# A two-layer decoder trunk: all four tiles of x transposed as loaded, two tiles loaded ahead of the weights, and zero matmuls in PE's waits

## The reference

```python
def rms_norm(x, g):
    y = x * lax.rsqrt(jnp.mean(x * x, axis=-1, keepdims=True) + 1e-6)
    return y * g

for i in range(2):
    hdn = rms_norm(x, norm_g[i])
    q, k, v, z = jnp.split(hdn @ w_in[i], 4, axis=-1)      # (1024, 4096)
    if i == 0:    # block-sparse attention with rotary; q and k normalised per head
        q = apply_rope(rms_norm(split_heads(q), a_q_norm), cos, sin)
        k = apply_rope(rms_norm(split_heads(k), a_k_norm), cos, sin)
        y = moba_attention(q, k, split_heads(v))
    else:         # attention with a forget-gate bias, no rotary
        y = forgetting_attention(q, k, v, log_sigmoid(f_logit))
    x = x + (merge_heads(y) * silu(z)) @ w_out[i]
```

## Time and profile before

| | before |
|---|---|
| median of 3 runs | 550.47 us (550.08 to 550.68) |
| the profiled execution | 551.01 us |
| its span, first to last instruction | 548.9 us |
| PE busy | 539.3 us, 98% of the span |
| DVE, ACT, POOL busy | 406.1, 291.2, 300.2 us |
| chain of waits that ended last | PE 93% of it |
| DMA | 50.09 MB, mean 91 GB/s |

### The profile page before, as it was taken

The page is one execution under the profiler, slowest core; times in us unless marked ns, Lnnn a source line. Parts: engine busy times, 40 slices in busy tenths (PEclk is TensorE's granted clock), DMA queues, the critical chain, the costliest instruction groups (busy, mean ns, idle before and its releaser), DMA issues.

```text
span 548.9 us, 9783 instructions
## 1 busy us (share of the span) xinstructions
PE 539.3 (98%) x2963; PEld 498.1 (91%) x2963; DVE 406.1 (74%) x1049; ACT 291.2 (53%) x863; POOL 300.2 (55%) x352
## 2 busy tenths in 40 slices
PE   5999999999999999999999999999999999999998
PEld 4989999999999999888888999999999999998887
DVE  2886999999999999964563778778787878788331
ACT  5846473737383828272454473838373737474400
POOL 4674555555555555452735486757574747476300
PEclk9999999999999999999999999999999999999999
DMA  8914314141313131324413335425141534232121
GB/s 252 256 14 116 116 39 116 38 116 38 115 38 115 43 110 57 96 80 122 114 40 79 96 97 78 113 61 130 46 131 44 121 57 122 72 102 80 36 96 59
DMA packets 78540, 50.09 MB, mean 91 GB/s; under 512 B 4256, under 2 KB 71720, under 8 KB 78512
## 3 DMA queue, kind: packets, MB, share of 16 engines
q1 hardware_dynamic: 78496, 49.74, 33.6%
q10 hardware_dynamic: 16, 0.00, 0.0%
HBM read 47.62 MB, written 2.11 MB: 91 GB/s over the span
## 4 chain that ended last, share of the span: by engine, by line
PE 93%; POOL 2%; ACT 1%; DMA 1%; DVE 1%; SPq 1%; issue 0%; POOLq 0%
PE banks L380 26%; PE banks L382 26%; PE banks L381 26%; PE banks L510 6%; PE banks L496 3%; PE banks L485 2%; PE banks L484 2%; PE banks L483 2%; DMA first_raw<-in_a_w_in_dram 1%; ACT hT_hi L677 1%; POOL w_lo L1180 1%; PE banks L417 1%; POOL rstd L1207 0%; DVE hT_lo L880 0%; PE banks L537 0%
## 5 line engine op out<-in xcount | busy, mean ns | idle before, releaser
L1180 POOL TENSOR_TENSOR w_lo<-w_raw,w_hi 128x512 fp32r<-128x512 f32 x147 | 189.6, 1303 | 82.7 <-ACT w_hi L645 82.7
L380 PE MATMUL banks<-w_hi,hT_hi 128*128 128x384 f32 x512 | 173.9, 340 | 1.2 <-DVE hT_lo L880 0.6
L381 PE MATMUL banks<-w_lo,hT_hi 128*128 128x384 f32 x512 | 171.8, 336 | 0.0
L382 PE MATMUL banks<-w_hi,hT_lo 128*128 128x384 f32 x512 | 171.8, 336 | 0.0
L966 DVE STREAM_TRANSPOSE banks<-qkn 32x256 f32<-32x256 f32 x240 | 109.4, 456 | 3.6
L380 PEld LDWEIGHTS banks<-w_hi,hT_hi 128*128 128x128 f32 x512 | 96.6, 189 | 3.8 <-POOL w_lo L1180 1.7
L381 PEld LDWEIGHTS banks<-w_lo,hT_hi 128*128 128x128 f32 x512 | 96.6, 189 | 0.6
L382 PEld LDWEIGHTS banks<-w_hi,hT_lo 128*128 128x128 f32 x512 | 96.5, 189 | 0.0
L691 ACT ACTIVATE junk<-banks 128x128 bf16<-128x128 f32 x128 | 34.1, 273 | 117.4 <-PE banks L382 117.4
L645 ACT ACTIVATE w_hi<-w_raw 128x512 fp32r<-128x512 f32 x148 | 89.1, 638 | 9.4 <-PE banks L382 5.4
L1032 DVE RECIPROCAL gz<-gz 128x128 f32<-128x128 f32 x64 | 54.4, 910 | 0.7 <-ACT gz L743 0.7
(11 more groups left out here) (120 smaller groups left out, 906.5 us busy)
## 6 DMA issues: line engine op xcount, KB each, us to landing
w_raw<-in_b_w_in_dram SPq DMA_DIRECT2D x64, 256.0 KB, 3.6
w_raw<-in_a_w_in_dram SPq DMA_DIRECT2D x52, 256.0 KB, 2.9
w_raw<-in_w_out_dram SPq DMA_DIRECT2D x32, 256.0 KB, 2.7
first_raw<-in_a_w_in_dram SPq DMA_DIRECT2D x12, 256.0 KB, 5.4
cos_t<-c_rows SPq DMA_DIRECT2D x8, 256.0 KB, 3.7
out_dram<-xs SPq DMA_DIRECT2D x7, 256.0 KB, 2.0
xs<-in_x_dram SPq DMA_DIRECT2D x3, 512.0 KB, 6.8
xs<-in_x_dram SPq DMA_DIRECT2D x2, 256.0 KB, 3.3
```

Of the source, the lines that this page charges most:

```text
L380: pe.matmul(dst, ah, bh, start=first and m == 0, stop=False)
L381: pe.matmul(dst, ah, bl, start=False, stop=False)
L382: mm = pe.matmul(dst, al, bh, start=False, stop=last and m == n - 1)
L1180: pool.tensor_tensor(w_lo[:, slot, k, :], raw, f32(w_hi[:, slot, k, :]), ALU.subtract).then_inc(wlo_set, by)
```

## The change

UNSCALED goes from 2 to 4: no tile of x is multiplied by r before its transposes, norm_x is gone from layer 0, r_rows has four columns, and scale_z covers 512 columns instead of 256. SP issues both halves of tile 0 and then tile 1 ahead of the first weights. PE transposes tiles 0 and 1 one after the other, with four and then five matmuls on the zeros of wf behind them (keep_busy, into PSUM bank 0, which the first real matmul overwrites), and then takes each chunk for both tiles. ACT turns to tile 0 before chunk 0. DVE takes w_lo of chunks 0, 3 and 5 instead of 3, 5 and 7, POOL 1, 2, 4, 6 and 7 instead of 0, 1, 2, 4 and 6. The folding of the sine tables moves wholly to POOL.

```diff
-UNSCALED = 2
+UNSCALED = 4
+ZEROS = KC * (LO_ROW + 8)
-POOL_FIRST = {0: 1, 1: 1, 2: 2, 4: 2, 6: 2}
-DVE_FIRST = (3, 5, 7)
+POOL_FIRST = {1: 2, 2: 1, 4: 2, 6: 2, 7: 1}
+DVE_FIRST = (0, 3, 5)
@@ SP
                 sp.dma_start(xs[:, 0, cols], x[0, 0:P, cols]).then_inc(x_half[half], 16)
-                load_first((half,))
             load_x(1)
-            load_first(range(2, 6))
+            load_first(range(6))
@@ PE
+            def keep_busy(count):
+                zeros = wf[:, :, :].rearrange("p k n -> p (k n)")
+                for _ in range(count):
+                    pe.matmul(banks[:, 0, 0:ZEROS], zeros[:, 0:P], zeros[:, 0:ZEROS], start=True, stop=True)
...
                     turn_hidden(layer, 0)
-                    first_w(0, 0)
-                    qkv_part(layer, 0, 0, 0, (0,))
+                    keep_busy(4)
                     turn_hidden(layer, 1)
-                    for k in (1, 2):
-                        first_w(0, k)
-                        qkv_part(layer, 0, 0, 0, (k,))
-                    qkv_part(layer, 0, 0, 1, range(3))
-                    for k in range(3, KC):
+                    keep_busy(5)
+                    for k in range(KC):
                         if k == KC - 1:
                             turn_hidden(layer, 2)
                         first_w(0, k)
@@ DVE
-                    norm_x(layer, 2)
-                    split_first_w(0, (7,))
                     split_hidden(layer, 2)
-                    norm_x(layer, 3)
-                    fold_tables()
+                    split_hidden(layer, 3)
+                    dve.wait_ge(tables_set, 1)
+                    fold_cosines()
                     split_v(layer, 0, 0, 0)
                     split_v(layer, 0, 0, 1)
-                    split_hidden(layer, 3)
```

More of the change, by code:

```diff
@@ L310, in load_second @@
                     load_chunk(w_raw[:, k, :], head_src(0, 1)(k), raw_in[k])
-                sp.wait_ge(wlo_set, 4)
-                sp.wait_ge(wlo_odd, 1)
+                sp.wait_ge(wlo_set, 3)
+                sp.wait_ge(wlo_odd, 2)
                 for k in range(RAW, KC):
@@ L747, in first @@
                     act.dma_start(gz[0:KC, 0, 0:P], norm_g[0].rearrange("(k n) -> k n", k=KC)).then_inc(gain_in[0], 16)
+                    act.wait_ge(gain_set, 1)
+                    split_hidden(layer, 0)
                     split_w(layer, 0, 0, (0,))
-                    act.wait_ge(gain_set, 1)
-                    split_half(layer, 0, 0)
+                    split_half(layer, 1, 0)
                     split_w(layer, 0, 0, (1,))
[L752 to L757, removed]
+                    split_half(layer, 1, 1)
+                    split_w(layer, 0, 0, range(2, KC))
+                    split_hidden(layer, 2)
                     square_x(layer, 0)
-                    square_x(layer, 3)
-                    split_hidden(layer, 2)
                     square_x(layer, 1)
+                    split_hidden(layer, 3)
                     read_qkv(layer, 0, 0, 0)
                     read_qkv(layer, 0, 0, 1)
-                    split_w(layer, 1, 1, (0, 1))
-                    split_hidden(layer, 3)
-                    split_w(layer, 1, 1, (2, 3, 4))
+                    for t in (2, 3):
+                        square_x(layer, t)
                     read_qkv(layer, 0, 0, 2)
+                    split_w(layer, 1, 1, range(5))
                     split_w(layer, 1, 1, (5,))
@@ L896, in split_first_w, with fold_cosines @@
                                       ALU.subtract).then_inc(wlo_odd, 1)
[L898 to L908, removed]
+            def fold_cosines():
                 for m in range(2):
@@ L1071, in first @@
                     split_hidden(layer, 0)
+                    split_first_w(0, (0,))
                     split_hidden(layer, 1)
                     split_first_w(0, (3, 5))
-                    norm_x(layer, 2)
-                    split_first_w(0, (7,))
                     split_hidden(layer, 2)
-                    norm_x(layer, 3)
-                    fold_tables()
+                    split_hidden(layer, 3)
+                    dve.wait_ge(tables_set, 1)
+                    fold_cosines()
                     split_v(layer, 0, 0, 0)
                     split_v(layer, 0, 0, 1)
-                    split_hidden(layer, 3)
-                    dve.wait_ge(tables_set, 3)
+                    dve.wait_ge(tables_set, 2)
                     dve.wait_ge(cos_set, 1)
@@ L1087, in first @@
                     norm_qk(layer, 0, 2)
-                    split_first_w(1, (3,))
+                    split_first_w(1, (0,))
                     split_v(layer, 0, 0, 3)
                     norm_qk(layer, 0, 3)
-                    split_first_w(1, (5, 7))
+                    split_first_w(1, (3, 5))
                     dve.wait_ge(wf_split, 1)
@@ L1097, in first @@
                     dve.tensor_scalar(cos_t[:, 0, 0, :], cos_t[:, 0, 0, :], SCALE, None, ALU.mult).then_inc(tables_set, 1)
-                    dve.wait_ge(tables_set, 4)
+                    dve.wait_ge(tables_set, 3)
                     split_v(layer, 0, 0, 0)
@@ L1224, in first @@
                     for k, by in POOL_FIRST.items():
-                        if k == 6:
-                            rstd_x(layer, 2)
                         split_w(layer, 0, 0, (k,), by=by)
-                    for t in (0, 3, 1):
+                    pool.wait_ge(tables_in, 64)
+                    pool.tensor_scalar(gains[:, 0, :], gains[:, 0, :], SCALE, None, ALU.mult).then_inc(tables_set, 1)
+                    for t in range(2):
                         rstd_x(layer, t)
+                    pool.wait_ge(tables_set, 1)
+                    half = P // 2
+                    for m in range(2):
+                        for a in range(2):
+                            folded = pool.tensor_tensor(sin_t[:, :, m, a * half:(a + 1) * half],
+                                                        sin_t[:, :, 1, a * half:(a + 1) * half],
+                                                        bcast(gains[:, m, (1 - a) * half:(2 - a) * half], TILES), ALU.mult)
+                    folded.then_inc(tables_set, 1)
                     rstd_qk(layer, 0, 0)
                     rstd_qk(layer, 0, 1)
[L1233 to L1239, removed]
+                    for t in (2, 3):
+                        rstd_x(layer, t)
                     rstd_qk(layer, 0, 2)
-                    for k, by in tuple(POOL_FIRST.items())[1:]:
+                    for k, by in POOL_FIRST.items():
                         if k == 4:
```

## The result

Over 20 runs the kernel after took 551.99 us in the median (550.25 to 552.76), the kernel before 550.58 us on the same chip: a ratio of 1.002, with a 95% interval of 1.0014 to 1.0026. The predicted 552.0 us was met, but not for the reason given. In 14 of the 20 runs the mean granted clock of TensorE was 0.997, and they took 551.76 to 552.76 us; in the other six it was 1.0, and they took 550.25 to 550.95 us, no more than before. The profiled execution (552.51 us, span 550.4, clock 0.997) is one of the 14, and it shows what lowers the mean: one stretch of 3.4 us at half clock near 40 us (half of 3.4 is 0.3% of the span). Of the runs without a profile only the mean clock is known, and I take 0.997 there for the same event.

The account below looks back on a forecast made before the run. A fixed PE block begins at T, set by POOL and DVE: 19.2 + 4.9 + 12.5 + 1.9 = 38.5, plus 1.6 of collisions, 40.1 against 38.62, so 1.5 us later: median 552.0 us, range 549.8 to 553.8.

Parts of the forecast that it names:

- T2 = 19.2 us (Part 1): Loads and zeros: PE turns to tile 2 of x at 19.2 us, against 20.20 before.
- The zeros at 0 to 0.5 us: Nine zero matmuls during PE's early waits cost nothing; lifting the clock gains 0 to 0.5 us, taken as 0.
- T: Start of the transposes of q and k of head 0, opening the fixed block; predicted 40.1 us against 38.62.
- ACT's row of T2 + 4.9: ACT's hT_hi of tile 2 and squares of tiles 0 and 1 end 4.9 us after PE turns to tile 2.
- POOL's row of 12.5 us and collisions of 1.6 us (Part 2): POOL's factors, sine pieces and low parts before T take 12.5 us; meetings with DVE add 1.6 us.
- the two cancel: Rival: only PE's lead or collision-free POOL and DVE holds, or half of each; T 37.5 to 39.7, 550.9 us, chance 0.30.
- Scale_z and r_row at 0 (Part 3): In the periods, scale_z over 512 columns, at most 0.86 us, is covered by slack; later r_rows cost nothing.
- The clock falls in PE's new pause: Rival: PE idles some 4 us from 35.8, returns at the lower clock, loses 1.9 us; 553.9 us, chance 0.08.

Follow-up runs that it names:

- experiment 2: The kernel after without the nine zero matmuls (keep_busy(4) and keep_busy(5)): 552.31 us, ratio 1.0032.
- experiment 1: The kernel after with 14 unread products of 384 columns filling PE's pause before the transposes of q and k: 550.74 us, ratio 1.0.
- experiment 3: The kernel after with the gains and q's half of the sine table made on DVE, POOL keeping k's half: 549.44 us, ratio 0.9978.
- experiment 8: The kernel of experiment 3 with one reciprocal of 176 columns on DVE ahead of norm_qk(3), lengthening PE's pause: 551.45 us.
- experiment 5: Experiment 3 with ACT reading the last tile's sums earlier, POOL's factor at once, DVE making three low parts of head 1: 549.02 us, ratio 0.9972.
- experiment 9: The kernel after with six unread products of 384 columns in the last part of PE's pause: 550.62 us.
- experiment 6: The kernel after with four unread products of 384 columns at the start of PE's pause: 552.01 us.
- held-up kernel before: The kernel before with 3.5 unread reciprocals on DVE ahead of its normalising of tile 3, giving PE a pause; run twice: 553.02 and 553.09 us.

## Why the prediction was right in its number and wrong in its reason

- **T2 = 19.2 us (Part 1): roughly right.** Measured 18.68. ACT's first high part, so chunk 0, starts at 8.20, not at 8.8, within the bounds given; the first products run at the upper level (0.33 us at 9.87) and wait for POOL's low parts, 0.79 us at 11.89. PE's lead over before is 1.5 us there, and z ends 2.4 us earlier than before (38.58 less the 2.68 of pause is 35.90; 38.62 less 0.28 is 38.34), as predicted, but in part by luck: PE needs 17.2 us from T2 to the end of z, not 16.6, which makes up for a T2 that came 0.5 us early. The working also names 20 products there; the trace has 18, and it is 18 that give its 16.6.
- **The zeros at 0 to 0.5 us: right, taken as 0.** Without them T2 and T are 0.01 and 0.02 us later (experiment 2). They do raise the clock before the first product, and those products wait for low parts all the same, as the prediction had it.
- **ACT's row of T2 + 4.9: right.** ACT's last sum of tile 1 ends at 23.56, T2 + 4.88.
- **POOL's row of 12.5 us and collisions of 1.6 us (Part 2): the step that failed.** Its rows:

```profile
23.64 0.19 POOL L1179 TENSOR_TENSOR msx<-ssx,eps 128x1 f32<-128x1 f32 x1
...
24.59 2.83 POOL L1223 TENSOR_TENSOR sin_t<-sin_t,gains 128x256 f32<-128x256 f32 x4
27.37 0.65 POOL L1194 TENSOR_TENSOR msq<-ssq,eps_raw 128x2 f32<-128x2 f32 x1
28.09 1.03 POOL L1196 TENSOR_TENSOR rstd<-msq,power 128x2 f32<-128x2 f32 x1
...
32.84 2.55 POOL L1169 TENSOR_TENSOR w_lo<-w_raw,w_hi 128x512 fp32r<-128x512 f32 x2
35.35 0.64 POOL L1194 TENSOR_TENSOR msq<-ssq,eps_raw 128x2 f32<-128x2 f32 x1
36.08 0.69 POOL L1196 TENSOR_TENSOR rstd<-msq,power 128x2 f32<-128x2 f32 x1
```

  From 23.64 to 36.77 it is 13.1 us, where 14.1 was predicted. And on DVE, what it met:

```profile
27.01 1.56 DVE L900 TENSOR_TENSOR cos_t<-cos_t,gains 128x512 f32<-128x512 f32 x2
...
34.56 1.39 DVE L894 TENSOR_TENSOR w_lo<-w_raw,w_hi 128x512 fp32r<-128x512 f32 x1
```

  The collisions are there and where they were put, but I priced each as a whole DVE instruction in POOL's way. The sine pieces were over 0.4 us after the first cosine piece began and took 2.83 for four; the small operations behind them lost 0.46 (0.65 for 0.19) and 0.33 (1.03 for 0.70), and the one beside DVE's low part 0.45: 1.2 us, not 1.6. The three factors of x behind it took 0.95 us each (23.64 to 24.59 the first), not 1.13, which is the other 0.6. With T2 0.5 us earlier, T came out at 38.58 and not at 40.1. This is the rival "the two cancel", with its price of 550.9 us; the six runs without the fall (median 550.5) are it. The rule of the Trainium skill ("SBUF — State Buffer", Who interferes with whom) on mutual exclusion agrees with these rows, if read as waiting out what is left of the other's instruction: 0.33 to 0.46 us here. That `norm_qk` disturbs POOL no row shows.
- **Scale_z and r_row at 0 (Part 3): right in effect.** In the first period scale_z takes 1.09 us, above the bound of 0.86 that I gave; the block from T on is as long as before wherever the clock holds (510.3 in experiment 1, 510.4 in experiment 3), so it is hidden.
- **"The clock falls in PE's new pause": weighed at 0.08 and true in 14 of 20 runs.** Its mechanism is the result; its price, 1.9 us, was near the 1.6 measured, and its base, T at 40.1, was the forecast's error. I took the case to need a pause of some 4 us, and had no row for less; the pause was 2.7, and in experiment 8 1.9 was enough. Nor is the fall where I put it, in the trace of the kernel after: PE comes back at the upper level, does its transposes in 1.09 us, and loses the clock 1.3 us after its return; in that of experiment 2 the fall lies in the pause, as I had it. The first half of the rule cited from the Trainium skill ("TensorE: Matmul & The Clock Gate", What's actually happening), that activity opens the gate, agrees with the zeros (first products at 0.33 us a matmul with them, at 0.52 without); the second, that an idle array closes it, agrees with the table above, where the falls come with the longer pauses, and with the trace of experiment 2. In the kernel after PE was at work again for 1.3 us before the clock fell; no run shows why.

So two errors of about 1.5 us, T too late and the clock taken as safe, cancelled. That the number came out is luck, and the ratio alone would have confirmed a wrong account.

## What to carry to other kernels

Time won for an engine that then waits for another chain is only a pause, and on TensorE a pause has a price of its own: in the kernels made from the kernel after, 1.9 us or more of it cost 1.6 us in most runs, about as much as PE's lead at tile 2. Shorten the chain that the engine waits for (experiments 3 and 5, 549.4 and 549.0 us) or, where it can't be shortened, put products into the pause so that no long idle stretch is left: 14 that fill it (experiment 1) and six at its end that leave 1.6 us (experiment 9) ended the falls, four at its start that leave 2.1 us (experiment 6) did not. Whether the end is a better place than the start for the same number of products was not tried. And where the chain of waits names an engine, look at the timelines too: in experiment 3 it named ACT, and POOL was the one without a pause. When runs of one kernel fall into two groups, look at the granted clock of each before explaining their median.

## What the runs showed of the hardware that was not expected

- The granted clock fell not in the pause but 1.3 us behind its end in the kernel after and 1.4 us in experiment 6, at 39.9 us in both although PE stopped 0.6 us apart; in experiment 2 it fell at 38.08, inside the pause, and was down when PE came back at 38.60. It stayed down for 3.4 us in all three traces.
- In the kernels made from the kernel after the step is sharp: 1.6 us idle, 0 of 21 runs; 1.9 us, 7 of 11; and 2.7 us no worse than that, 14 of 20. In the held-up kernel before, 2.3 us gave 2 of 10.
- scale_z took 1.09 us for 512 columns, against 0.43 us for 256 columns: 2.5 times the time for twice the columns. Its second input also changed its stride, from every second element to every fourth; which of the two did it was not tried.
